# Hybrid attention and DeltaNet layer: gate masks, query loads and DeltaNet steps at other places in the order

## The reference

```python
mod = silu(c) @ W_ada + b_ada                      # 6 vectors of 1024: shift, scale, gate, twice
h = rmsnorm(x, norm1_g) * (1 + sc1) + sh1
proj = h @ W_in                                     # columns: qa ka va | qkvb | zb bb ab | ga gb
ya = chunk_band_attention(qa, ka, va, rel_table)    # 8 heads x 64, chunks of 64, 9 chunks wide
yb = gated_deltanet(qkvb, zb, bb, ab, ...)          # 4 heads x 128, causal conv of 4 taps, delta rule
merged = sigmoid(ga) * (ya @ W_A) + sigmoid(gb) * (yb @ W_B)
x = x + gt1 * (merged @ W_out)
h = rmsnorm(x, norm2_g) * (1 + sc2) + sh2
gate, up = split(h @ W_ffn_in);  x = x + gt2 * ((silu(gate) * up) @ W_ffn_out)
return rmsnorm(x, final_g)
```

## Time and profile before

| | us |
|---|---|
| median of 3 runs | 1871.59 |
| lowest, highest | 1869.07, 1871.85 |
| the profiled execution | 1867.37 |
| its span, first to last instruction | 1865.7 |
| PE (TensorE) busy in the span | 1775.3 |
| DVE, ACT, POOL busy | 892.4, 473.4, 164.4 |
| mean granted TensorE clock | 0.972 of full |

### The profile page before, as it was taken

How to read it: one execution, slowest core, us unless ns; L and a number is a source line. 1 busy time by engine, 2 the same in 40 slices (tenths; PEclk the granted TensorE clock), 3 DMA queues, 4 the chain that set the end, 5 groups by cost and what they waited for, 6 DMA issues and landing times.

```text
span 1865.7 us, 22580 instructions
## 1 busy us (share of the span) xinstructions
PE 1775.3 (95%) x8387; PEld 1424.8 (76%) x8387; DVE 892.4 (48%) x1231; ACT 473.4 (25%) x861; POOL 164.4 (9%) x208
## 2 busy tenths in 40 slices
PE   5998879999999999999899979999999999999997
PEld 5876768888767777677678868888888888888876
DVE  6675566667534444444554344243333324333336
ACT  3334422222243333343321222111111111111101
POOL 1125551111001001010000000000000000000000
PEclk7899999999999999999999979999999999999998
DMA  7745555666423231340445110222022012102002
GB/s 246 213 117 171 173 167 181 180 183 187 130 76 108 74 82 65 91 129 34 163 165 192 54 53 26 65 68 57 12 67 66 29 40 67 56 11 67 23 0 102
DMA packets 208877, 186.13 MB, mean 100 GB/s; under 512 B 15481, under 2 KB 186618, under 8 KB 208826
## 3 DMA queue, kind: packets, MB, share of 16 engines
q1 hardware_dynamic: 201770, 160.01, 29.2%
q0 software_dynamic: 7056, 25.43, 3.5%
HBM read 140.58 MB, written 44.83 MB: 99 GB/s over the span
## 4 chain that ended last, share of the span: by engine, by line
PE 78%; DVE 4%; issue 2%; DMA 1%; ACT 1%; SPq 0%; DVEq 0%; ACTq 0%; POOLq 0%
PE pm L895 35%; PE ps L895 17%; PE pm L1220 12%; PE aT L1089 3%; PE aS L1112 3%; PE aT L1100 1%; PE gps L1034 1%; DVE asc L1765 1%; DVE a_raw L1763 1%; ACT w_hi L1267 1%; DMA yst<-yb_d 1%; PE pm L1184 1%; PE gps L1039 0%; DVE tmp L1886 0%; DVE xT L1947 0%
## 5 line engine op out<-in xcount | busy, mean ns | idle before, releaser
L1547 DVE TENSOR_TENSOR w_lo<-w_raw,w_hi 128x1024 fp32r<-128x1024 f32 x105 | 131.2, 1250 | 536.8 <-ACT w_hi L1267 525.7
L895 PE MATMUL pm<-act_hi,w_hi 128*128 128x512 f32 x832 | 257.4, 391 | 4.0 <-DVE act_lo L1596 4.0
L895 PE MATMUL pm<-act_lo,w_hi 128*128 128x512 f32 x832 | 257.3, 391 | 0.0
L895 PE MATMUL pm<-act_hi,w_lo 128*128 128x512 f32 x832 | 256.6, 390 | 0.0
L895 PE MATMUL ps<-act_hi,w_hi 128*128 128x512 f32 x720 | 253.7, 434 | 0.7 <-DVE est L1649 0.7
L1267 ACT ACTIVATE w_hi<-w_raw 128x1024 fp32r<-128x1024 f32 x105 | 110.7, 1055 | 503.4 <-PE pm L895 492.4
L895 PE MATMUL ps<-act_lo,w_hi 128*128 128x512 f32 x720 | 228.0, 398 | 0.0
L895 PE MATMUL ps<-act_hi,w_lo 128*128 128x512 f32 x720 | 226.2, 396 | 0.0
L895 PEld LDWEIGHTS pm<-act_hi,w_hi 128*128 128x128 f32 x832 | 156.5, 188 | 36.8 <-issue 4.2
L895 PEld LDWEIGHTS pm<-act_lo,w_hi 128*128 128x128 f32 x832 | 156.7, 188 | 33.0
L895 PEld LDWEIGHTS pm<-act_hi,w_lo 128*128 128x128 f32 x832 | 156.5, 188 | 33.1
(11 more groups left out here) (277 smaller groups left out, 2108.4 us busy)
## 6 DMA issues: line engine op xcount, KB each, us to landing
w_raw<-in_w_in_dram SPq DMA_DIRECT2D x45, 512.0 KB, 5.4
w_raw<-in_w_ffn_in_dram SPq DMA_DIRECT2D x44, 512.0 KB, 3.8
a_raw<-in_w_ada_dram SPq DMA_DIRECT2D x32, 512.0 KB, 4.1
f_raw<-in_w_ffn_out_dram SPq DMA_DIRECT2D x22, 512.0 KB, 4.3
adab<-in_w_ada_dram SPq DMA_DIRECT2D x8, 1024.0 KB, 7.8
pk_d<-pk SPq DMA_DIRECT2D x8, 768.0 KB, 3.9
qkva_d<-est POOLq DMA_DIRECT2D x12, 512.0 KB, 4.4
ast<-qkva_d SPq DMA_DIRECT2D x24, 256.0 KB, 6.2
```

What stands on the lines that cost most here:

```text
L895: ins = pe.matmul(dst[:, cols], wt[:, ds % 2, k, :], at[:, cols], start=(first and n == 0), stop=(last and n == 2))
L1547: dve.tensor_tensor(w_lo[:, ds % 2], w_raw[:, ds % NR], w_hi[:, ds % 2].bitcast(F32), ALU.subtract)\
```

## The change

Three things are moved; no instruction of a compute engine and no DMA is added or taken away.

1. POOL in units 6 to 9: the masked gates of block t + 2 come right behind the causal product of block t, ahead of the scaled products and of the store of a convolved unit. They stood at the end of the unit's list.
2. SP: the query loads of blocks 4 and 5 come ahead of the store of unit 10's convolution instead of behind it. They still wait for query steps 0 and 1.
3. The DeltaNet steps: slots 1, 3, 5, 7, 9, 11, 13, 15, 18, 20, 22, 24, 26 in both loops become 4, 6, ..., 28 in the first and 2, 4, ..., 26 in the second, on PE, ACT, DVE and POOL alike. POOL's order of instructions stays the same.

```diff
-        GSLOT = [1, 3, 5, 7, 9, 11, 13, 15, 18, 20, 22, 24, 26]
-        Q_AT = {s: q for q, s in enumerate(GSLOT)}
+        Q_AT_A = {4 + 2 * q: q for q in range(NQ)}
+        Q_AT_B = {2 + 2 * q: q for q in range(NQ)}
...
             load_unit(D_A, 0, w_in_v, C_QA)
+            for t in (4, 5):
+                load_pre(t, 0)
             store_conv(10)
-            for t in range(4, NT):
+            for t in (6, 7):
                 load_pre(t, 0)
...
             for d in range(D_PRE, D_PRE + 4):
                 a = 2 * (d - D_PRE)
-                causal(a)
-                causal(a + 1)
+                for t in (a, a + 1):
+                    causal(t)
+                    if t + 2 < NT:
+                        masked_gates(t + 2)
                 scaled(a)
                 store_conv(d - 1)
                 scaled(a + 1)
-                if a + 2 < NT:
-                    masked_gates(a + 2)
-                    masked_gates(a + 3)
...
-                    if s in Q_AT:
-                        gdn_step(i, Q_AT[s])
+                    if s in Q_AT_A:
+                        gdn_step(i, Q_AT_A[s])
                     unit_k(D_A + s // 8, i, s % 8, ps[(D_A + s // 8) % 2])
```

More of the change, by code:

```diff
@@ L835, in _, with gdn_slot @@
             solve(range(BLK - 1))
-            def gdn_slot(t, s):
-                q = Q_AT.get(s)
+            def gdn_slot(t, q):
                 if q == Q_TO:
@@ L861, in _ @@
                 for s in range(32):
-                    gdn_slot(i, s)
+                    gdn_slot(i, Q_AT_A.get(s))
                     if s in (13, 21, 29):
@@ L871, in _ @@
                 for s in range(32):
-                    gdn_slot(i + 4, s)
+                    gdn_slot(i + 4, Q_AT_B.get(s))
                     if s in (13, 21, 29):
@@ L1137, in _ @@
                     attention_slot(i, s)
-                    if s in Q_AT:
-                        gdn_step(i + 4, Q_AT[s])
+                    if s in Q_AT_B:
+                        gdn_step(i + 4, Q_AT_B[s])
                     unit_k(D_B + s // 8, i, s % 8, ps[(D_B + s // 8) % 2])
@@ L1427, in _ @@
                         evac(D_A + s // 8 - 1, i, "copy")
-                    if s in Q_AT:
-                        gdn_read_act(i, Q_AT[s])
+                    if s in Q_AT_A:
+                        gdn_read_act(i, Q_AT_A[s])
                 evac(D_A + 3, i, "z")
@@ L1464, in _ @@
                     attention_act(i, s)
-                    if s in Q_AT:
-                        gdn_read_act(i + 4, Q_AT[s])
+                    if s in Q_AT_B:
+                        gdn_read_act(i + 4, Q_AT_B[s])
                     exp_act(i, s)
@@ L1772, in _ @@
                 for s in range(32):
-                    if s in Q_AT:
-                        gdn_dve(i, Q_AT[s])
+                    if s in Q_AT_A:
+                        gdn_dve(i, Q_AT_A[s])
                     if s % 8 == 0 and s:
@@ L1837, in _ @@
                             scores_dve(i, m)
-                    if s in Q_AT:
-                        gdn_dve(i + 4, Q_AT[s])
+                    if s in Q_AT_B:
+                        gdn_dve(i + 4, Q_AT_B[s])
                     if s % 8 == 0 and s:
```

## The result

| | before | after |
|---|---|---|
| median, us | 1870.76 (7 runs) | 1879.16 (7 runs) |
| lowest, highest | 1869.07, 1872.05 | 1875.87, 1880.68 |
| ratio, 95% interval | | 1.0044, 1.0035 to 1.0054 |
| the profiled execution, its span | 1867.37, 1865.7 | 1880.4, 1878.8 |
| mean granted clock | 0.972 | 0.970 |

The change makes the kernel 8.4 us slower. The two profiled executions differ by 13.0 us: that of before lies 3.4 under its median, that of after 1.2 over its own.

The account below looks back on a forecast made before the run. PE, busy 95% of the span, was taken to bound the kernel, with its waits. Terms -6.5 + 1.6 + 3.0 + 4.8 - 0.2 + 1.2 - 1.1 gave +2.8 on 1871.6: 1874.4 us, range 1865 to 1881.

Parts of the forecast that it names:

- the most likely case: Whole kernel: the summed forecast of +2.8 us, to 1874.4, called no change that counts; chance 0.41.
- rival C: First loop: loads held behind Q_TV land late and delay slot 19, 1 to 1.5 us per turn, +5 us; chance 0.18.
- part 1, masks: Units 7 to 9: removed gate waits come back before block 3's keys; gain 0, bounds -0.6 and +1 us.
- part 2, queries: Query steps 4 and 5: earlier load brings step 5 from 235.85 to 229.2, -6.6 us.
- head of the first loop on a low clock: After the first `mod` product: Q_TO and Q_GQ work now runs behind it on a low clock, +1.6 us.
- period, three turns: First loop: each turn grows from 57.99 to 59.0 us, +3.0 for three; bounds +0.6 and +2.
- clock behind three waits: First loop, slot 3: three new 2.7 us waits each cost 1.6 us of clock, +4.8, between 0 and 5.
- last turn: First loop's last turn, product to end: 50.8 us, before 51.0, so -0.2 us.
- wait for the heads: Start of the second loop: PE waits longer for head loads sent behind the last Q_KY, +1.2 us.
- The ring of stores: Units 7 to 9: exponentials wait for earlier blocks' stores, setting the pace without the masked gates; gain 0.
- Rival A: Units 7 to 9: gate waits stay removed, 7.3 + 1.6 us come off, 1865.5; chance 0.23.
- the contention: Head of the first loop: DVE's weight split beside POOL's solve takes back 0.1 us.

Follow-up runs that it names:

- e2: Kernel before with only the masked gates on POOL moved earlier; 1869.28 us, ratio 0.9994.
- e1: Kernel before with only the query loads of blocks 4 and 5 put ahead of the store; 1866.03 us, ratio 0.9975.
- e6: Changed kernel, with SP loading the turn's fourth-unit weights and fifth `a_raw` ahead of the DeltaNet loads that wait for Q_TV; 1868.38 us, ratio 0.9991.
- e3: Kernel before with only the first loop's DeltaNet steps moved, to slots 4 to 28; 1888.09 us, ratio 1.0092.
- e12: Changed kernel with only the weights' load ahead of the state's load on SP, `a_raw` left behind it; 1868.83 us, ratio 0.9986.
- e4: Kernel before with only the second loop's DeltaNet steps moved, to slots 2 to 26; 1869.49 us, ratio 0.9992.
- e5: Changed kernel with the first loop's DeltaNet steps back at their old slots; 1863.12 us, ratio 0.9962.
- e9: Changed kernel with e6's edit and the `mod` products of groups 0 and 1 at the ends of slots 6 and 8; 1860.33 us, ratio 0.9942.
- e8: Changed kernel with e6's edit and the `mod` product of group 0 at the end of slot 6, not 3; 1860.79 us, ratio 0.9954.

## Why the prediction was right or wrong

The interval holds the result, the sign of the most likely case doesn't: +2.8 was forecast as no change that counts, and +8.4 was measured. What came is rival C, which was given 1879.4 and 0.18. That its figure lies 0.2 us from the measured one is luck: the late loads cost twice what it was priced with, and part 1, the clock, the period and the last turn took the rest off again.

| term | predicted | measured | from |
|---|---|---|---|
| part 1, masks | 0 (-0.6 to +1) | -1.3 (-1.5 in the traces) | e2 |
| part 2, queries | -6.6, 0.1 back to the solve | -6.5, 2.0 back; in all -4.6 | e1 |
| head of the first loop on a low clock | +1.6 | +1.6 in e6 (8.72 - 7.12), +1.9 in after, +3.0 in e3 | first product to the next |
| period, three turns | +3.0 | +2.0 | e6, clock taken off |
| clock behind three waits | +4.8 (0 to 5) | +1.6 in e6, +2.9 in after, +6.2 in e3 | product to product |
| last turn | -0.2 | -0.6 | e6 |
| wait for the heads | +1.2 | +1.5 in e6, +2.5 in after | waits, against the 3.4 of before |
| late weights and `a_raw` | 0 (rival C: +5) | +10.3 to +10.8 | e12, e6 |
| second loop | -1.1 | -1.1 | e4 |

**Right.** Part 2's gain at the query steps, 6.5, by the mechanism given: step 4 at 224.29, then the convolution, as the 0.34 us of wait for est behind it shows. PE stands at the first slot 3 instead (13.1 us, where 11.6 was worked out; the solve's 2 us are most of the difference), so the wait of 8.3 us for Q_GQ really was worth next to nothing: from query step 0 to that product it took 46.15 us in the changed kernel and 46.72 in e5, which has the old slots. The wait for the heads varies by more than its term: it was 3.4 to 5.1 us in the five kernels with the old slots in the first loop, and 4.9 to 5.9 in after, e3, e6 and e12; the means are 1.2 apart, as forecast. The chain of DVE from the state update to the next product was given as 13.66 and took 320.16 - 306.48 = 13.68. A turn was given as 59.0, or 60.6 with the clock; with the weights early it took 60.4 and then 58.6 twice. That DVE holds it is shown by e9.

**Wrong, the step that matters.** The bound of the period said "+2 if the weights of the turn's fourth unit, issued behind the read of Q_TV three slots later, land late", and rival C priced that at 1 to 1.5 us a turn by the products at slot 19. The place and the cause were right, and the paths were not followed to their ends. The prediction counted from the load to ACT's split to DVE's split to slot 19. It didn't ask what is queued behind the split on ACT: the read of Q_Y5, for which Q_U6 in slot 18 waits, one slot before the product at slot 19. It named the `a_raw` behind the same load and put no price on it. Nor did it add the clock that such a wait costs. In the kernel after, turns 0 to 3 lost, beyond those of e6, 1.8, 3.7, 2.6 and 1.8 us between the products of groups 3 and 5, 10.0 in all; e6 and e12 put it at 10.8 and 10.3. The 3.7 and 2.6 are the turns in which Q_U6 waited; the two of 1.8 came by slot 19, as the rival had it, but with `a_raw` last and above its 1 to 1.5. The landing was also worse than the 5.5 us at which slack ended: these weights landed 6.5, 7.9, 7.7 and 6.5 us after their issue, and 5.4 to 5.8 in before and in e12.

**Wrong, part 1.** The ring of stores was taken as fixed in time. It holds as predicted, and it still turned 1.5 us faster with the masks early. Rival A, by which the 7.3 us stay removed, is excluded; of its cause, stores that land sooner, some is there. The last of block 1's small stores, on which the exponential of block 3 waits, landed 3.3 to 4.2 us after its issue in the four kernels with the masks late, and 2.0 in after, e2, e5, e6, e8 and e12, though, counted from the matmuls over the gates, it was issued up to 1.0 us later there. Why is open; no run takes that apart.

**Wrong, the contention.** 0.1 us was counted for the weight split beside POOL's solve, and none for the norms' chain, which the same move of 6.5 us puts beside longer solve rows. It measured 2.0.

**Wrong in size, the clock.** 4.8 was at the upper end of its range; 1.6 came in e6, 2.9 in the kernel after and 6.2 in e3, which is beyond the range, as are e3's 3.0 at the head (bounds 1.5 and 2.2). These are single executions, and no run shows what sets the clock apart between them; the sum below takes e6's value and leaves the other 1.3 to the late loads. The forecast is low by 5.6. Of that, the late loads explain +10.5, the contention +2.0, the heads +0.3, and against them stand part 1 with -1.3 and the clock, the period and the last turn with 3.2 + 1.0 + 0.4 less: +6.9, more by 1.3 than was measured, of which 0.5 is within what the medians of before differ by and the rest stays open.

## What to carry to other kernels

When a step is moved later, walk every queue that waits for its reader: first what stands behind that wait on the issuing engine (here the weights behind `next_gst`), then what stands behind the late data's first consumer (here a 0.6 us read behind ACT's split), until the walk comes back to the busiest engine. Bind loads to the earliest event that frees their buffer, not to a neighbour's place in the queue; that one line of order was worth 10 us of the 16 here. A wait that is removed is worth only what the next late thing lets through, so look for that before counting it: PE's 8.3, the 1.39 and the heads' 6.6 us came back, whole or in part, as waits for DVE.

## What the runs showed of the hardware

- The granted clock fell behind some waits of 1.4 to 2.7 us and not behind others of the same length at the same place: 7.12, 8.67 and 10.06 us for the same work (after and e6).
- Small DVE operations with two inputs in SBUF (128x64) take the length of the POOL operation beside them: 0.65 us beside steps of 0.64, 0.42 beside shorter ones; a chain of fourteen was 2.0 us longer.
- Large ones too: a weight split (128x1024) of 1.22 us took 3.36 beside two of POOL's masks and 1.38 without them, and a multiplication of 1.22 took 3.82 to 4.03 beside POOL's `Ct` of 2.53. The reduction of a `mod` group (L1765, one input) took 2.00 beside `Ct` in the kernel before, within the 1.87 to 2.03 that it takes everywhere.
- The same load lands at other times by its place in the queue: the `a_raw` of the fifth group took 8.8 to 9.0 us from issue to landing in the kernel after, 0.6 us behind the weights, and 5.7 to 7.3 in e12 without them there. Weight loads of 512 KB between 264 and 490 us had a median of 5.2 us before and 6.5 after; their longest was 5.8 before and 7.9 after, but also 8.2 in e6 and e12, where it cost nothing.
